# Column sums by products with ones, a longer run of idle-filling products, and four subtractions moved from VectorE to GpSimd

## The chip, the cores and the metric

The kernel runs on one core of one Trainium2 chip. The metric is the device time of one execution in microseconds; lower is better. The engines are named as in the profile: PE is TensorE (PEld its weight loads), DVE is VectorE, ACT is ScalarE, POOL is GpSimd, and SP is the queue that issues most DMAs.

## What is computed

One residual decoder layer on 1024 tokens of width 1024, all in float32. Only its front is touched by the change:

```python
mod = (c_act @ w_ada[l] + b_ada[l])[:, None, :]
sh1, sc1, g1, sh2, sc2, g2 = jnp.split(mod, N_MOD, axis=-1)
h = rms_norm(h_res, norm1_g[l]) * (1.0 + sc1) + sh1
proj = h @ w_in[l]          # columns: q 512 | k 128 | v 128 | u 512
...                         # q, k, v: windowed attention; u: pooling means
h_res = h_res + g1 * mixed
h2 = rms_norm(h_res, norm2_g[l]) * (1.0 + sc2) + sh2
ff = jnp.square(jax.nn.relu(h2 @ w_mlp_in[l])) @ w_mlp_out[l]
h_res = h_res + g2 * ff
```

## The kernel before

The order of every engine's work is written out by hand; semaphores join the engines. Nothing is reordered by a scheduler: an instruction that waits holds up all that stands behind it on its engine.

**The modulation.** The vector c is laid out as 128 partitions by 8. The loop over `n` on DVE adds 16 pieces of `w_ada` (128x1024 each, one `add_piece` per piece, L1164 and L1166): the first eight into `acc` (shift, sh1), the other eight into `squares` (scale, sc1, the last of them in two halves, L1206). Each piece arrives by a DMA from SP. What is then missing is the sum over the 128 partitions. `turn_sums` on PE transposes `acc` or `squares` in 128x128 blocks into PSUM (L1965), and DVE sums each block along its rows by TENSOR_REDUCE (L1219 for the shift, L1226 for each half of the scale, inside `scale_1`) and adds the bias columns `cols` (L1221, L1228). L1231 forms `a1 = (1 + scale) * norm_g`.

**The input.** ACT scales the first two 128-token tiles of x (`xh`, L709), PE transposes each (`turn_x`, 8 transposes), DVE and ACT apply `a1` and `b1` to one half each (`make_h` L1240, `make_h_half` L718), ACT rounds the result to `fp32r` (`hi_h` L728) and DVE subtracts to get the low part (`lo_h` L1246). The weights are split in the same way: ACT casts (`hi_wu` L733 for the four pieces of the u columns, 128x1024 each; `hi_wqkv` L737 for the eight pieces of the q, k, v columns, 128x768 each), and DVE subtracts (`lo_wu` L1253, `lo_wqkv` L1259). Every projection is three products, hi*hi, hi*lo and lo*hi (L1969 to L1971), per 128 rows of weights.

**The order on PE.** `turn_sums(acc)`, `keep_clock(8)`, `turn_x(0)`, `turn_x(1)`, `keep_clock(6)`, `turn_sums` for each half of `squares`, `keep_clock(14)`, then `project_u(0)` (24 products; its steps wait for `h_lo` and, two steps each, for one `wu_lo`), the q projection (24 products, step k waits for `wqkv_lo` k+1), the k and v projection, and `project_u(1)`. `keep_clock(n)` is n products of `ident` by `ident` into a PSUM bank that nobody reads; each is two records in the trace, while a transpose is one.

**The order on DVE behind the modulation.** `scale_1(0)`, `make_h(0,0)`, `scale_1(1)`, `lo_wu(0)`, `lo_h(0,0)`, `lo_wu(1)`, `lo_h(0,1)`, `lo_wu(2)`, `lo_wu(3)`, four `lo_wqkv`, `make_h(1,0)`, four `lo_wqkv`, two `lo_h` of the second tile. **On ACT:** `hi_wu(0)`, `hi_wu(1)`, `hi_h(0,0)`, `make_h_half(0)`, `hi_h(0,1)`, `hi_wu(2)`, `hi_wu(3)`, five `hi_wqkv`, `make_h_half(1)`, and so on. **On POOL:** masks and pooling bands, the root for the first two tiles (L1823, L1825), then nothing until the q and k norms of the first tile.

Of the kernel before, what the change touches and what calls it, by code (L numbers as in the profile page):

```python
# [16 lines left out]
P = 128  # L17
F32 = mybir.dt.float32
# [3 lines left out]
ALU = mybir.AluOpType  # L22
ACT = mybir.ActivationFunctionType
AX_X = mybir.AxisListType.X
# [11 lines left out]
SH1, SC1, G1, SH2, SC2, G2 = range(6)  # L36
# [17 lines left out]
def build(nc, x, c, positions, w_ada, b_ada, norm1_g, w_in, q_norm_g, k_norm_g, attn_sinks,  # L54
          pool_w, pool_scale, w_o, norm2_g, w_mlp_in, w_mlp_out, out):
    S, D = x.shape[1], x.shape[2]
    IN = w_in.shape[2]
# [9 lines left out]
    KD = D // P  # L67
# [5 lines left out]
    QKV = AW + 2 * KVW  # L73
# [11 lines left out]
    with ExitStack() as ctx:  # L85
# [3 lines left out]
        def sb(name, shape, dt=F32):  # L89
            return ctx.enter_context(nc.sbuf_tensor(name, shape, dt))  # L90
# [4 lines left out]
        def over(name, shape, at, dt=F32):  # L95

            with ExitStack() as hold:
                if at:
                    hold.enter_context(nc.sbuf_tensor(name + "_below", [P, at // 4], F32))
                return hold.enter_context(nc.sbuf_tensor(name, shape, dt))  # L100

        ident = sb("ident", [P, P])
        ones = sb("ones", [P, P])
        small = sb("small", [P, 256])
        cols = sb("cols", [P, 72])
        a1, b1, a2, b2 = (small[:, 8 * j:8 * j + 8] for j in range(4))
# [23 lines left out]
        acc = over("acc", [P, D], AT_ACC)  # L130


        with ExitStack() as mix_ctx:
# [4 lines left out]
            wih = mb("w_in_hi", [P, KD, IN], F32R)  # L138
            wil = mb("w_in_lo", [P, KD, IN], F32R)
# [66 lines left out]
        psum = ctx.enter_context(nc.psum_tensor("psum", [P, 8, 512], F32))  # L206
# [4 lines left out]
        def bank(j):  # L211
            return psum[:, j, :]

        def banks(j):
            return psum[:, j:j + 2, :].rearrange("p b n -> p (b n)")
# [52 lines left out]
        mod_turned = sem("mod_turned")  # L268
        sc1_turned = sem("sc1_turned")
        mod_taken = sem("mod_taken")  # L270

        a1_ready = sem("a1_ready")
        wu_hi, wu_lo = sem("wu_hi"), sem("wu_lo")
# [180 lines left out]
        def landed(eng, piece):  # L454

            n = place[piece]
            buf, use, _ = buffer_of(n)
            eng.wait_ge(raw_in[buf], 16 * use)
            return piece_at(n)
# [54 lines left out]
        acc_sc = squares[:, :]  # L514
# [634 lines left out]
        def _(dve):  # L1149
            own_d = Chain(dve, own["dve"])  # L1150
            v = nc.vector
# [43 lines left out]
            for n in range(2 * KD):  # L1195
                if n >= 1:
                    dve.wait_ge(mod_summed, n)
                if n < KD:
                    add_piece(acc[:, :], ("sh1", n), n, mod_summed)
                elif n < 2 * KD - 1:  # L1200
                    add_piece(acc_sc, ("sc1", n - KD), n - KD, mod_summed)
                else:
                    a = landed(dve, ("sc1", KD - 1))
                    for h in range(2):
                        cut = slice(512 * h, 512 * h + 512)
                        v.scalar_tensor_tensor(out=acc_sc[:, cut], in0=a[:, cut], scalar=silu[:, KD - 1:KD],  # L1206
                                               in1=acc_sc[:, cut], op0=ALU.mult, op1=ALU.add).then_inc(mod_summed, 1)
                if n == 4:
                    dve.wait_ge(rows_in, 16 * 4)
                    v.tensor_copy(rows[64:72, :], posi[64:72, :]).then_inc(posf_ready, 1)  # L1210
                if n == KD + 2:

                    dve.wait_ge(rows_turned, 1)
                    v.tensor_copy(cols[:, :], psum[:, 4, 0:72]).then_inc(cols_ready, 1)
                if n == 2 * KD - 4:

                    dve.wait_ge(cols_ready, 1)
                    dve.wait_ge(mod_turned, 1)
                    v.tensor_reduce(b1, banks(0).rearrange("p (k n) -> p k n", n=P), AX_X, ALU.add).then_inc(mod_taken, 1)  # L1219
                    dve.wait_ge(mod_taken, 1)  # L1220
                    own_d.step(v.tensor_tensor(b1, b1, cols[:, 8 * SH1:8 * SH1 + 8], ALU.add))  # L1221
            def scale_1(h):

                c4 = slice(4 * h, 4 * h + 4)
                dve.wait_ge(sc1_turned, h + 1)
                own_d.step(v.tensor_reduce(a1[:, c4], bank(2 + h).rearrange("p (k n) -> p k n", n=P), AX_X, ALU.add))  # L1226
                own_d.wait()
                own_d.step(v.tensor_tensor(a1[:, c4], a1[:, c4],  # L1228
                                           cols[:, 8 * SC1 + 4 * h:8 * SC1 + 4 * h + 4], ALU.add))
                own_d.wait()  # L1230
                v.scalar_tensor_tensor(out=a1[:, c4], in0=a1[:, c4], scalar=1.0, in1=cols[:, 48 + 4 * h:52 + 4 * h],  # L1231
                                       op0=ALU.add, op1=ALU.mult).then_inc(a1_ready, 1)
# [14 lines left out]
                                xh[:, t % 2, 512 * h:512 * h + 512].rearrange("p (k n) -> p k n", n=P),  # L1247
                                hT(t)[0][:, 4 * h:4 * h + 4, :].bitcast(F32), ALU.subtract).then_inc(h_lo, 1)

            def lo_wu(j):  # L1250
                a = landed(dve, ("wu", j))
                dve.wait_ge(wu_hi, j + 1)
                v.tensor_tensor(wil[:, 2 * j:2 * j + 2, QKV:IN], a.rearrange("p (k n) -> p k n", k=2),  # L1253
                                wih[:, 2 * j:2 * j + 2, QKV:IN].bitcast(F32), ALU.subtract).then_inc(wu_lo, 1)

            def lo_wqkv(k):
                a = landed(dve, ("wqkv", k))
                dve.wait_ge(wqkv_hi, k + 1)
# [2 lines left out]
            scale_1(0)  # L1261
            make_h(0, 0)
            scale_1(1)
            lo_wu(0)
            lo_h(0, 0)
            lo_wu(1)
            lo_h(0, 1)
            lo_wu(2)
            lo_wu(3)
            for k in range(4):  # L1270
                lo_wqkv(k)
            make_h(1, 0)
# [491 lines left out]
        def _(pool):  # L1764
            own_p = Chain(pool, own["pool"])
            g = nc.gpsimd
# [64 lines left out]
            pool.wait_ge(x_squared, 2)  # L1831
            root(rx[:, 0:2], ssx[:, 0:2], D, x_root)

            def lo_wo(k):
                pool.wait_ge(wo_hi, k + 1)
                g.tensor_tensor(wol[:, k, :], piece_at(place[("wo", k)]), woh[:, k, :].bitcast(F32),
                                ALU.subtract).then_inc(wo_lo_pool, 1)
# [123 lines left out]
        def _(pe):  # L1961
            mm = nc.tensor.matmul
# [16 lines left out]
            def keep_clock(n, at):  # L1979

                for _ in range(n):
                    mm(psum[:, at, 0:P], ident[:, :], ident[:, :], start=True, stop=True)

            def turn_sums(o, sums):

                for k in range(o.shape[1] // P):
                    ins = tr(o[:, k * P:(k + 1) * P], sums[:, k * P:(k + 1) * P])
                return ins
# [114 lines left out]
            tr(psum[:, 4, 0:72], rows[0:72, :], 72).then_inc(rows_turned, 1)  # L2103

            pe.wait_ge(mod_summed, KD)
            turn_sums(banks(0), acc).then_inc(mod_turned, 1)
            pe.wait_ge(mod_summed, 2 * KD - 5)
            keep_clock(8, 2)
            turn_x(0)
            pe.wait_ge(cols_ready, 1)  # L2110
            turn_x(1)
            keep_clock(6, 2)
            for h in range(2):
                pe.wait_ge(mod_summed, 2 * KD + h)
                turn_sums(bank(2 + h), acc_sc[:, 512 * h:512 * h + 512]).then_inc(sc1_turned, 1)
            pe.wait_ge(mod_taken, 1)
            keep_clock(14, 0)

# [216 lines left out]
            for h in range(2):  # L2335
                if h == 1:
                    pe.wait_ge(h2_lo_last, 2)
                for b in range(2):
                    for c_ in ("C12", "C22"):
                        ins = head_half(b, c_, "A" + c_[1] + str(h + 1), late, NK * h, h == 0, h == 1)  # L2340
# [5 lines left out]
            for b in range(HEAD, NBLK):  # L2346
                for name in UP_NEXT:
                    up_product(b, name)
                    n = b - HEAD - KD - 1
# [56 lines left out]
```

## Time and profile before

| | us |
|---|---|
| three runs | 964.04, 964.57, 966.05 |
| median | 964.57 |
| the profiled execution, own time | 966.11 |
| its span in the trace | 964.4 |
| PE busy | 925.0 (96%) |
| DVE busy | 657.4 (68%) |
| ACT busy | 492.3 (51%) |
| POOL busy | 352.6 (37%) |

The profiled execution's own time lies 1.7 above its span and 1.5 above the median. A matmul's end is modelled in the trace, so a busy PE may still wait; its starts are what to read. In a row, the time before the bracket is the group's start and how long it lasted from its first start to its last end; the bracket holds the engine's idle time just before it and who ended that.

### The profile page before, as it was taken

The numbers are of one execution on the slowest core, as the hardware profiler recorded it, in microseconds if no ns is written. First come the engines' busy times: TensorE is split into PE (matmuls) and PEld (weight loads), VectorE is DVE, ScalarE is ACT, GpSimd is POOL, SyncE is SP. The second block draws the span as 40 slices with busy tenths as digits, with TensorE's granted clock in tenths as the row PEclk, the third lists the DMA queues.
The fourth block names the chain that finished last, engine by engine and source line by source line (L and its number), as shares of the span: only waits on it lengthen the run. The fifth ranks groups of instructions, "written<-read, shape, count | busy, mean of one in ns | idle before, by whom it ended". The sixth has DMA issues, their size and how long they took to land.

```text
span 964.4 us, 12633 instructions
## 1 busy us (share of the span) xinstructions
PE 925.0 (96%) x4411; PEld 765.2 (79%) x4411; DVE 657.4 (68%) x1000; ACT 492.3 (51%) x874; POOL 352.6 (37%) x342
## 2 busy tenths in 40 slices
PE   1898999998999999999999999999999999999998
PEld 1787788886778888787888788888888888888887
DVE  6876887878644687665556544535786666779896
ACT  1656777778464564644554455454443444333331
POOL 8032222215232443988888877851000000000000
DMA  9852332214222240665456533538999637987673
GB/s 360 298 170 93 131 110 79 78 64 153 89 88 87 88 154 22 222 213 176 154 169 210 177 132 133 173 138 276 351 345 333 226 99 239 308 307 245 227 252 113
DMA packets 92271, 175.54 MB, mean 182 GB/s; under 512 B 9320, under 2 KB 26288, under 8 KB 92208
## 3 DMA queue, kind: packets, MB, share of 16 engines
q1 hardware_dynamic: 92096, 174.70, 53.1%
q8 instruction: 35, 0.57, 0.2%
q14 instruction: 28, 0.23, 0.1%
q10 hardware_dynamic: 112, 0.04, 0.0%
HBM read 136.95 MB, written 37.75 MB: 181 GB/s over the span
## 4 chain that ended last, share of the span: by engine, by line
PE 84%; DVE 6%; ACT 5%; POOL 3%; issue 2%; DVEq 0%; POOLq 0%; ACTq 0%
PE psum L1969 26%; PE psum L1971 25%; PE psum L1970 25%; PE psum L1965 3%; ACT probs L780 2%; PE psum L2045 1%; PE psum L2068 1%; ACT probs L788 1%; POOL band L1788 1%; PE psum L2095 1%; PE psum L2026 1%; PE psum L2023 1%; PE psum L2024 1%; ACT qT L799 1%; DVE probs L1297 1%
## 5 line engine op out<-in xcount | busy, mean ns | idle before, releaser
L1076 ACT CAST down_operands<-down_raw 128x1024 fp32r<-128x1024 f32 x96 | 100.9, 1054 | 153.4 <-PE psum L1971 58.1
L1969 PE MATMUL psum<-down_operands 128*128 128x512 f32 x448 | 174.3, 389 | 0.0
L1970 PE MATMUL psum<-down_operands 128*128 128x512 f32 x448 | 174.3, 389 | 0.0
L1971 PE MATMUL psum<-down_operands 128*128 128x512 f32 x448 | 174.3, 389 | 0.0
L1705 DVE TENSOR_TENSOR down_operands<-down_raw,down_operands 128x1024 fp32r<-128x1024 f32 x93 | 112.5, 1219 | 19.1 <-ACT down_operands L1076 18.5
L1969 PE MATMUL psum<-h2T,w_operands 128*128 128x512 f32 x272 | 107.5, 395 | 1.9 <-DVE act_quads_a L1649 1.3
L1971 PE MATMUL psum<-h2T,w_operands 128*128 128x512 f32 x272 | 105.9, 390 | 0.0
L1970 PE MATMUL psum<-h2T,w_operands 128*128 128x512 f32 x272 | 105.9, 389 | 0.0
L1921 POOL TENSOR_TENSOR w_operands<-raw,w_operands 128x512 fp32r<-128x512 f32 x56 | 83.2, 1487 | 42.1 <-ACT w_operands L1028 42.1
L1969 PEld LDWEIGHTS psum<-down_operands 128*128 128x128 f32 x448 | 84.1, 188 | 17.6
L1970 PEld LDWEIGHTS psum<-down_operands 128*128 128x128 f32 x448 | 84.1, 188 | 17.4
L1971 PEld LDWEIGHTS psum<-down_operands 128*128 128x128 f32 x448 | 84.1, 188 | 17.3
L1823 POOL TENSOR_SCALAR small<-small 128x1 f32<-128x1 f32 (+2 forms) x23 | 8.3, 359 | 169.1 <-DVE small L1366 131.7
L1971 PE MATMUL psum<-t_sums_hi,w_operands 128*128 128x512 f32 x168 | 65.4, 389 | 0.0
L1969 PE MATMUL psum<-t_sums_hi,w_operands 128*128 128x512 f32 x168 | 65.4, 389 | 0.0
L1970 PE MATMUL psum<-t_sums_lo,w_operands 128*128 128x512 f32 x168 | 65.4, 389 | 0.0
L1969 PE MATMUL psum<-w_in_hi,hT_hi 128*128 128x512 f32 (+1 forms) x168 | 61.7, 368 | 2.7 <-DVE hT_lo L1246 1.7
L1969 PEld LDWEIGHTS psum<-h2T,w_operands 128*128 128x128 f32 x272 | 51.1, 188 | 15.8 <-issue 3.8
L1921 POOL TENSOR_TENSOR w_operands<-w_sums,w_operands 128x512 fp32r<-128x512 f32 x42 | 55.9, 1343 | 11.8 <-ACT w_operands L1028 11.8
L1970 PEld LDWEIGHTS psum<-h2T,w_operands 128*128 128x128 f32 x272 | 51.1, 188 | 10.8 <-issue 0.5
L1971 PE MATMUL psum<-w_in_hi,hT_lo 128*128 128x512 f32 (+1 forms) x168 | 59.6, 355 | 0.0
L1971 PEld LDWEIGHTS psum<-h2T,w_operands 128*128 128x128 f32 x272 | 51.1, 188 | 10.7
(251 smaller groups left out, 1973.4 us busy)
## 6 DMA issues: line engine op xcount, KB each, us to landing
down_raw<-in_w_mlp_out SPq DMA_DIRECT2D x160, 256.0 KB, 4.3
down_raw<-act_scratch SPq DMA_DIRECT2D x112, 256.0 KB, 3.3
raw<-in_w_ada SPq DMA_DIRECT2D x32, 512.0 KB, 4.7
raw<-in_w_mlp_in SPq DMA_DIRECT2D x32, 512.0 KB, 4.9
act_scratch<-act_quads_a SPq DMA_DIRECT2D x64, 256.0 KB, 2.2
act_scratch<-act_quads_b SPq DMA_DIRECT2D x48, 256.0 KB, 3.6
slots<-in_w_ada SPq DMA_DIRECT2D x8, 512.0 KB, 10.5
xh<-in_x SPq DMA_DIRECT2D x8, 512.0 KB, 6.1
```

Source lines behind the costliest of these rows:

```text
L780: nc.scalar.activation(pr[:, kv, h, 0:w], pr[:, kv, h, 0:w], ACT.Exp, bias=negm[:, hh:hh + 1], scale=rq(i)[:, hh:hh + 1], accum_out=den[:, ...
L788: ins = nc.scalar.activation(pr[:, kv, h, 0:w], pr[:, kv, h, 0:w], ACT.Copy, scale=rden[:, kv * G + h:kv * G + h + 1])
L799: nc.scalar.copy(qT[r, :, :].rearrange("p (m e) q -> p m e q", e=2)[:, :, e, :], bank(1)[r, :].rearrange("p (m q) -> p m q", q=P))
L1076: nc.scalar.copy(o[:, 0, :, :], r[:, 0:2, :]).then_inc(op2_hi, 1)
L1297: ins = v.tensor_tensor_reduce(out=pr[:, kv, h, 0:w], in0=banks(4)[:, 256 * h:256 * h + w], in1=mask[:, m0:m0 + w], scale=1.0, scalar=-3e3 ...
L1705: v.tensor_tensor(o[:, 1, :, :], r[:, 0:2, :], f32(o[:, 0, :, :]), ALU.subtract).then_inc(op2_lo_dve, 1)
L1788: own_p.step(g.affine_select(out=cut, in_=cut, compare_op=ALU.is_ge, fill=0.0, base=base, pattern=[[1, n]], channel_multiplier=-1))
L1921: g.tensor_tensor(o[:, 1, :, :], quad, o[:, 0, :, :].bitcast(F32), ALU.subtract).then_inc(w1_lo, 1)
L1965: return nc.tensor.transpose(o, i, ident[0:rows_, 0:rows_])
L1969: mm(o, wh, ah, start=first, stop=False, skip_group_check=adds)
L1970: mm(o, wh, al, start=False, stop=False, skip_group_check=adds)
L1971: return mm(o, wl, ah, start=False, stop=last, skip_group_check=adds)
```

## The change

Four things are done.

- `column_sum` takes the place of `turn_sums` at the front: for each block of 128 columns one product with the block as the stationary operand and one column of `ones` as the moving one, which leaves the sums over the partitions in one PSUM column. DVE's three TENSOR_REDUCE go, and the bias is added straight from PSUM.
- DVE copies `cols` behind piece 7 instead of piece 10.
- On PE, `keep_clock(8)` ahead of `turn_x(0)` becomes `keep_clock(14)`, and `keep_clock(6)` behind `turn_x(1)` becomes `keep_clock(4)`.
- The four `lo_wu` go from DVE, where they stood between `scale_1(1)` and `lo_wqkv(0)`, to POOL, behind the root of the first two tiles.

```diff
-                if n == KD + 2:
+                if n == KD - 1:
                     dve.wait_ge(rows_turned, 1)
                     v.tensor_copy(cols[:, :], psum[:, 4, 0:72]).then_inc(cols_ready, 1)
...
-                    v.tensor_reduce(b1, banks(0).rearrange("p (k n) -> p k n", n=P), AX_X, ALU.add).then_inc(mod_taken, 1)
-                    dve.wait_ge(mod_taken, 1)
-                    own_d.step(v.tensor_tensor(b1, b1, cols[:, 8 * SH1:8 * SH1 + 8], ALU.add))
+                    v.tensor_tensor(b1.rearrange("p (h k) -> p h k", h=2), psum[:, 0:2, 0:4],
+                                    cols[:, 8 * SH1:8 * SH1 + 8].rearrange("p (h k) -> p h k", h=2),
+                                    ALU.add).then_inc(mod_taken, 1)
             def scale_1(h):
...
-                own_d.step(v.tensor_reduce(a1[:, c4], bank(2 + h).rearrange("p (k n) -> p k n", n=P), AX_X, ALU.add))
-                own_d.wait()
-                own_d.step(v.tensor_tensor(a1[:, c4], a1[:, c4],
+                if h == 0:
+                    dve.wait_ge(mod_taken, 1)
+                own_d.step(v.tensor_tensor(a1[:, c4], psum[:, 2 + h, 0:4],
                                            cols[:, 8 * SC1 + 4 * h:8 * SC1 + 4 * h + 4], ALU.add))
...
             scale_1(1)
-            lo_wu(0)
             lo_h(0, 0)
-            lo_wu(1)
             lo_h(0, 1)
-            lo_wu(2)
-            lo_wu(3)
...
             root(rx[:, 0:2], ssx[:, 0:2], D, x_root)
+            def lo_wu(j):
+                a = landed(pool, ("wu", j))
+                pool.wait_ge(wu_hi, j + 1)
+                g.tensor_tensor(wil[:, 2 * j:2 * j + 2, QKV:IN], a.rearrange("p (k n) -> p k n", k=2),
+                                wih[:, 2 * j:2 * j + 2, QKV:IN].bitcast(F32), ALU.subtract).then_inc(wu_lo, 1)
+            for j in range(KD // 2):
+                lo_wu(j)
...
+            def column_sum(o, sums, k):
+                return mm(o, sums[:, k * P:(k + 1) * P], ones[:, 0:1], start=True, stop=True)
...
-            turn_sums(banks(0), acc).then_inc(mod_turned, 1)
+            for k in range(KD):
+                ins = column_sum(psum[:, k // 4, k % 4:k % 4 + 1], acc, k)
+            ins.then_inc(mod_turned, 1)
             pe.wait_ge(mod_summed, 2 * KD - 5)
-            keep_clock(8, 2)
+            keep_clock(14, 2)
             turn_x(0)
             pe.wait_ge(cols_ready, 1)
             turn_x(1)
-            keep_clock(6, 2)
+            keep_clock(4, 2)
             for h in range(2):
                 pe.wait_ge(mod_summed, 2 * KD + h)
-                turn_sums(bank(2 + h), acc_sc[:, 512 * h:512 * h + 512]).then_inc(sc1_turned, 1)
+                for k in range(4):
+                    ins = column_sum(psum[:, 2 + h, k:k + 1], acc_sc, 4 * h + k)
+                ins.then_inc(sc1_turned, 1)
```

On PE, at the front of the program, before the change (xh is the scaled input, squares the scale sums, ident the identity):

```order
L1965 MATMUL psum<-ident,acc 128x128 x8
L1982 MATMUL psum<-ident 128x128 x8
L1965 MATMUL psum<-ident,xh 128x128 x16
L1982 MATMUL psum<-ident 128x128 x6
L1965 MATMUL psum<-ident,squares 128x128 x8
L1982 MATMUL psum<-ident 128x128 x14
```

and after it:

```order
L1984 MATMUL psum<-ones,acc 128x1 x8
L1981 MATMUL psum<-ident 128x128 x14
L1964 MATMUL psum<-ident,xh 128x128 x16
L1981 MATMUL psum<-ident 128x128 x4
L1984 MATMUL psum<-ones,squares 128x1 x8
L1981 MATMUL psum<-ident 128x128 x14
```

Six more products of `ident` stand ahead of the transposes of x, two fewer behind them, and the transposes of the sums are products of one column.

On DVE, from the bias of the shift to the first weights of q, k and v, the piece of the difference:

```order
-L1219 TENSOR_REDUCE small<-psum 128x8
-L1221 TENSOR_TENSOR small<-small,cols 128x8
+L1219 TENSOR_TENSOR small<-psum,cols 128x8
 L1166 SCALAR_TENSOR_TENSOR squares<-raw,small,squares 128x1024 x2
 L1206 SCALAR_TENSOR_TENSOR squares<-raw,small,squares 128x512 x2
-L1226 TENSOR_REDUCE small<-psum 128x4
-L1228 TENSOR_TENSOR small<-small,cols 128x4
+L1228 TENSOR_TENSOR small<-psum,cols 128x4
 L1231 SCALAR_TENSOR_TENSOR small<-small,cols 128x4
 L1240 TENSOR_SCALAR xh<-psum,small 128x128 x4
```

The reduces are gone. What follows `scale_1(1)` was, before:

```order
L1231 SCALAR_TENSOR_TENSOR small<-small,cols 128x4
L1253 TENSOR_TENSOR w_in_lo<-slots,w_in_hi 128x2x512
L1246 TENSOR_TENSOR hT_lo<-xh,hT_hi 128x512
L1253 TENSOR_TENSOR w_in_lo<-slots,w_in_hi 128x2x512
L1246 TENSOR_TENSOR hT_lo<-xh,hT_hi 128x512
L1253 TENSOR_TENSOR w_in_lo<-slots,w_in_hi 128x2x512 x2
L1259 TENSOR_TENSOR w_in_lo<-slots,w_in_hi 128x768 x4
```

and is now:

```order
L1231 SCALAR_TENSOR_TENSOR small<-small,cols 128x4
L1246 TENSOR_TENSOR hT_lo<-xh,hT_hi 128x512 x2
L1253 TENSOR_TENSOR w_in_lo<-slots,w_in_hi 128x768 x4
```

On POOL, the root of the first two tiles, and behind it the four moved subtractions ahead of the q and k roots:

```order
L1813 TENSOR_SCALAR small<-small 128x2
L1815 TENSOR_TENSOR small<-small 128x2
L1827 TENSOR_TENSOR w_in_lo<-slots,w_in_hi 128x2x512 x4
L1813 TENSOR_SCALAR small<-small 128x10
L1815 TENSOR_TENSOR small<-small 128x10
```

## Rows read from the trace of the kernel before

**Rows 1.** The page: busy time, share and instructions of the engines.
```profile
PE 925.0 (96%) x4411; PEld 765.2 (79%) x4411; DVE 657.4 (68%) x1000; ACT 492.3 (51%) x874; POOL 352.6 (37%) x342
```

**Rows 2.** Timeline of PE: start, us, operation, count, idle before and its releaser.
```profile
22.38 3.78 PE L1982 MATMUL psum<-ident 128*128 128x128 f32 x16 [4.08 <-DVE squares L1166]
26.80 3.68 PE L1965 MATMUL psum<-ident,xh 128*128 128x128 f32 x16 [0.64 <-ACT xh L709]
30.26 1.96 PE L1982 MATMUL psum<-ident 128*128 128x128 f32 x12
32.06 1.04 PE L1965 MATMUL psum<-ident,squares 128*128 128x128 f32 x8
32.94 3.29 PE L1982 MATMUL psum<-ident 128*128 128x128 f32 x28
37.97 0.50 PE L1969 MATMUL psum<-w_in_hi,hT_hi 128*128 128x512 f32 x1 [1.75 <-DVE hT_lo L1246]
...
47.60 0.50 PE L1969 MATMUL psum<-w_in_hi,hT_hi 128*128 128x512 f32 x1 [0.93 <-DVE w_in_lo L1259]
```

**Rows 3.** Windows: busy us (records) by engine, PE clock column, DMA share, GB/s.
```profile
30.00:31.00 1.00, 1.00 (x7) 1.00 (x6) 0.28 (x1) 0.90 (x1) 0.00 (x0) 1.00 1.06 389
31.00:32.00 1.00, 1.00 (x10) 1.00 (x10) 0.00 (x0) 0.14 (x1) 0.00 (x0) 1.00 1.06 395
```

**Rows 4.** Chain that ended last, 32 to 52 us: start, us, what.
```profile
32.70 0.70 DVE small L1226
...
33.62 0.17 DVE small L1231
...
33.82 1.36 DVE xh L1240 x4
...
38.37 1.90 ACT w_in_hi L733 x2
...
48.10 0.23 PE psum L1970
```

**Rows 5.** Timeline of DVE and ACT around the first tile.
```profile
24.89 1.22 DVE L1219 TENSOR_REDUCE small<-psum 128x8 f32<-128x1024 f32 x1
...
30.10 1.04 ACT L733 CAST w_in_hi<-slots 128x1024 fp32r<-128x1024 f32 x1 [0.31 <-DMA slots<-in_w_in]
...
36.21 1.51 ACT L718 ACTIVATE xh<-psum,small 128x128 f32<-128x128 f32 x4 [0.37 <-DVE small L1231]
37.75 0.62 ACT L728 CAST hT_hi<-xh 128x512 fp32r<-128x512 f32 x1
...
39.57 2.35 DVE L1253 TENSOR_TENSOR w_in_lo<-slots,w_in_hi 128x1024 fp32r<-128x1024 f32 x2
41.84 3.56 DVE L1259 TENSOR_TENSOR w_in_lo<-slots,w_in_hi 128x768 fp32r<-128x768 f32 x4
45.32 1.36 DVE L1240 TENSOR_SCALAR xh<-psum,small 128x128 f32<-128x128 f32 x4
46.60 3.55 DVE L1259 TENSOR_TENSOR w_in_lo<-raw,w_in_hi 128x768 fp32r<-128x768 f32 x4
```

**Rows 6.** Timeline, 222 to 242 us: POOL subtractions of 128x1024 beside DVE.
```profile
222.31 2.38 POOL L1836 TENSOR_TENSOR w_o_lo<-raw,w_o_hi 128x1024 fp32r<-128x1024 f32 x1 [0.44 <-ACT w_o_hi L810]
222.75 2.02 DVE L1348 TENSOR_TENSOR pooledT<-pooledT,carry 128x64 f32<-128x64 f32 x1 [1.79 <-ACT pooledT L850]
...
234.84 1.22 DVE L1332 TENSOR_TENSOR w_o_lo<-raw,w_o_hi 128x1024 fp32r<-128x1024 f32 x1
235.35 2.96 POOL L1836 TENSOR_TENSOR w_o_lo<-raw,w_o_hi 128x1024 fp32r<-128x1024 f32 x1 [1.44 <-ACT w_o_hi L810]
...
238.71 2.40 POOL L1836 TENSOR_TENSOR w_o_lo<-raw,w_o_hi 128x1024 fp32r<-128x1024 f32 x1 [0.41 <-ACT w_o_hi L810]
239.15 1.29 DVE L1282 TENSOR_TENSOR pT_lo<-psum,pT_hi 128x512 fp32r<-128x512 f32 x2 [0.61 <-ACT pT_hi L764]
240.58 1.60 DVE L1332 TENSOR_TENSOR w_o_lo<-raw,w_o_hi 128x1024 fp32r<-128x1024 f32 x1
```

More of the change, by code:

```diff
@@ L1248, in lo_h @@
                                 hT(t)[0][:, 4 * h:4 * h + 4, :].bitcast(F32), ALU.subtract).then_inc(h_lo, 1)
[L1250 to L1254, printed above, removed]
             def lo_wqkv(k):
```

## The prediction

> **What bounds the kernel now.** I read the busy times first: PE is busy 96% of the span and all others far less [rows 1], so time is won only where PE stands idle. The change touches the first 50 us alone, so I read PE's timeline there [rows 2]. Once the input projections begin at 37.97, PE has one gap left before 51: at 47.60, 0.93 us, ended by DVE's `lo_wqkv(4)`. From there the q projection follows DVE's last four subtractions, which end at 46.60 + 3.55 = 50.15 [rows 5]; behind them PE needs one more step, and then has its k, v and second u projections ready to run. So the end of `lo_wqkv(7)`, 50.15, is the point that matters: whatever moves it moves the rest. The chain of waits says the same: DVE's reduce and small operations, `make_h`, ACT's casts, then DVE's subtractions [rows 4, 5]. I call M the start of `make_h(0,0)`, 33.82 before [rows 4].
>
> **The column sums.** Each half of the scale now costs PE 4 products of two records, 8 in all, where 4 transposes stood. A transpose at the fast level takes (32.94 - 32.06)/8 = 0.11 [rows 2]. No row has a product with one moving column; its weight load is that of the neighbours, so 0.11 per record is my upper bound (0.9 per half, 0.45 more than before) and half of it the lower one, since less is streamed. I take 0.11. DVE loses the reduce of 0.70 ahead of M [rows 4] and one of 0.61 behind it; the 1.22 of the shift [rows 5] lies ahead of DVE's last pieces of the scale, which then end at 29.2 instead of 30.3. PE isn't there before 30, so that is worth nothing. The earlier copy of `cols` costs nothing either: it is the same 0.2 us on DVE, which waits for pieces there.
>
> **The clock.** The window table's clock column reads 1.00 all along and doesn't show it, the pace of the records does. Before: 16 transposes from 26.80 to 30.26, 0.216 each; 8 from 32.06, 0.11 each [rows 2]; the records per us go from 7 to 10 and 12 about 31.2 [rows 3]. 128 columns in 0.11 are the 2.4 GHz level, 0.216 for the same work 1.2 GHz. Before the rise PE had worked since 26.80 without a break (4.4 us), and since 22.38 with a break of 0.64. Now 28 records start at 22.38 and nothing breaks the run. I bound the rise by these two: 26.8, as long behind the start as it was behind the break, and 31.2, no earlier than before. I claim no fixed length; I take 26.8, as the break is what the change takes away. Then 20 records are slow (to 26.8) and 8 fast (27.6); 16 transposes at 0.11 end at 29.4, 8 records of `keep_clock(4)` at 30.2, 8 of the column sums at 31.1. Before, DVE began 0.3 behind the last transpose's start; the bias addition would start at 31.4 and L1231 0.2 later, at 31.6, against 33.62. For each us that the clock rises later, it comes about 0.5 later.
> The Trainium skill ("TensorE: Matmul & The Clock Gate", Part 4: PE-mode transpose) says that transposes don't count as activity for the clock. This trace speaks against it: of the 4.4 us before the rise, 3.5 were transposes. By the page the rise would hang on the `ident` products alone, of which there are more now; the sum above would stay.
>
> **The moved subtractions, and who they block.** POOL takes 2.38 and 2.40 for such a subtraction [rows 6]; DVE took 1.2. The point is what runs beside it. At 222.75 a DVE operation on 64 elements per partition, both inputs in SBUF, lasts 2.02: it ends when POOL's, begun at 222.31, ends (224.7). At 240.58 another lasts 1.60 instead of the 1.22 of its like at 234.84. The reverse too: POOL's operation at 235.35 lasts 2.96, as DVE's of 234.84 was running. DVE's operations at 239.15, with one input in PSUM, run at their usual 0.65 beside POOL [rows 6]. So DVE operations with two SBUF inputs and POOL's subtractions take turns. In `scale_1` that is L1231; and all of `lo_h` and `lo_wqkv`.
> First piece: ACT's cast ends at 29.8, POOL holds from 29.85 to 32.25. L1231 (asked for at 31.6) waits until 32.25, then POOL's second piece starts (its cast is done at 31.14 [rows 5]) and holds until 34.5. M becomes 32.3, 1.5 earlier than 33.82. `make_h(0,0)` 1.36 to 33.7; the second L1231, wanted at 33.9, waits until 34.5. ACT: `make_h_half` 1.5 to 36.05, cast 0.62 to 36.7, `hi_wu(2)` to 37.65, `hi_wu(3)` to 38.6 (1.90 for both [rows 4]), then the q, k, v casts at 0.75 to 0.8 (three quarters of 1.04 [rows 5]).
> From 37.7 on POOL and DVE share the lock: POOL's third piece to 40.1; `lo_wqkv(0)`, ready at 39.4, to 40.9; POOL's fourth, 2.25 of it held, to 43.15; `lo_wqkv(1)` to (3) at 0.8 to 0.9 each, 45.65; `make_h(1,0)` 1.36 to 47.0; the last four 3.55 [rows 5], to **50.5**. Against 50.15: 0.35 later. The 1.5 won at M, and the 4 x 1.2 taken off DVE, go to two POOL pieces held at 2.3 each and to ACT's casts, which are in no greater hurry than before (DVE now idles from 37.4 to 39.4, where it worked). `project_u(0)` waits for the fourth piece at 43.15 and ends at 43.15 + 6 x 0.23 (a product of 512 columns [rows 4]) = 44.6, 3 us before the q projection's fifth step needs its weights: covered. Past that nothing changes: behind the moved pieces POOL waits for the squares of q and k, which come after the q projection; and on SP's queue no load of x, parameters or modulation waits for `wu_lo`.
> The skill's page "SBUF — State Buffer" (Who interferes with whom) gives this as an exclusive lock of a whole instruction, for DVE operations with two SBUF inputs. It leaves the sum as it is.
>
> **Sum.** Span 964.4 + 0.35, own time 966.11 + 0.35; the profiled execution stands 1.54 above the median, so 964.57 + 0.35 = **964.9**. A measurement tells about 0.2%, 1.9 us, from no change.
>
> **Rival 1, slower: POOL's second piece gets ahead of L1231.** If DVE asks later than 32.25, POOL already holds for its second piece, and L1231 waits until 34.6. M is then 34.65, 2.35 later than in my forecast; the second L1231 no longer waits (0.6 saved at 34.5), which leaves `lo_wqkv(7)` at 50.5 + 1.85 = 52.35, 2.2 later than before: 966.8. It decides at a request of 32.25, that is a clock rise at 28.1 or later by the 0.5 per us. For it: the rise before came at 31.2, and my 26.8 rests on one instance. Against it: 1.3 us of margin, more if the column sums are cheaper. If the clock had not risen by 31.2 either, it would also be this case. Chance 0.26, of which about 0.17 come out over 1.9.
>
> **Rival 2, faster: no turns are taken.** If these POOL operations (rows of two strips of 512) don't block DVE, M is 31.8, `make_h_half` starts at M + 2.05, `hi_wu(2)` ends at M + 5.1 = 36.9, POOL's pieces at 36.9 + 2 x 2.4 = 41.7, and PE is bound by them: 6 products of `project_u(0)` (1.4) and 24 of q (5.5) end at 48.6, against 51.2: 2.6 earlier, 962.0. Against it stand the three pairs of [rows 6] with two SBUF inputs on DVE. Chance 0.08.
>
> **Rival 3: the turns cost less.** If POOL's hold is 1.9 instead of 2.3 (the 1.60 at 240.58 shows 0.15 released early) and casts keep pace, the result is 0.5 to 1.5 better than before: 963.1 to 964.1. Chance 0.16, in "same" nearly all.
>
> **Rival 4: the clock drops.** PE now idles 38.0 to 40.1 and 41.5 to 43.15, against 1.75 at most before, without a drop. If it fell, 18 products until 48 at 0.43 instead of 0.23 would cost 3.6, less the 0.7 of cover: 2.9, 967.8. Chance 0.04.
>
> **The numbers.** My forecast holds 0.46: 964.9, itself 964.2 to 965.6. Together: faster 0.10 (rival 2 and the edge of 3), slower 0.22 (rivals 1 and 4, and 0.01 of the rest), same 0.68. For 8 in 10 the range takes in rival 3 and most of rival 1 and leaves out rival 2 and the far end: 962.9 to 967.0.
>
> **What would show it.** In the changed trace: the pace of PE's records falls from 0.216 to 0.11 at about 26.8, within the first stretch of 28 or the transposes (else rival 1); the first L1231 lasts about 0.6 instead of 0.17 and ends with POOL's first piece, the second likewise with POOL's second; M at 32.3 or 34.6; `lo_wqkv(0)` lasts 1.5 or more; the last `lo_wqkv` ends at 50.5; PE's records from 51 on are shifted by the same amount as that end. I am wrong if DVE's operations beside POOL keep their lengths (rival 2), or if what follows 51 us takes up or returns a shift, for which I see no place.

## The result

Fourteen runs of each kernel: before 965.16 us median (964.04 to 966.52), changed 966.93 us median (966.63 to 969.21). The ratio is 1.0023 with a 95% interval of 1.0016 to 1.003: the change makes the kernel about 2.2 us slower (2.2 by the means of the fourteen, 1.8 by the medians). Eight of the changed kernel's runs lie between 966.63 and 966.97, the other six between 967.59 and 969.21. Forecast was 964.9 and no measurable difference, in a range of 962.9 to 967.0.

The profile of the changed kernel (own time 966.97, span 965.2). Page, part 1, which answers to [rows 1]:

```profile
PE 928.3 (96%) x4435; PEld 768.0 (80%) x4435; DVE 653.6 (68%) x993; ACT 492.1 (51%) x874; POOL 364.2 (38%) x346
```

PE's timeline at the front, which answers to [rows 2] (start, length of the group, count, idle before and its releaser):

```profile
22.45 5.80 PE L1981 MATMUL psum<-ident 128*128 128x128 f32 x28 [2.64 <-DVE squares L1166]
28.17 2.21 PE L1964 MATMUL psum<-ident,xh 128*128 128x128 f32 x16
30.21 1.06 PE L1981 MATMUL psum<-ident 128*128 128x128 f32 x8
31.11 1.84 PE L1984 MATMUL psum<-ones,squares 128*128 128x1 f32 x16
...
40.76 0.47 PE L1968 MATMUL psum<-w_in_hi,hT_hi 128*128 128x512 f32 x1 [1.83 <-POOL w_in_lo L1827]
...
43.72 0.80 PE L1968 MATMUL psum<-w_in_hi,hT_hi 128*128 128x512 f32 x1 [0.42 <-POOL w_in_lo L1827]
...
51.83 0.28 PE L1968 MATMUL psum<-w_in_hi,hT_hi 128*128 128x256 f32 x1
```

The 16 transposes of x take 2.21 instead of 3.68: the faster pace is there before they begin. PE now waits for POOL twice. The last row is the first product for k and v.

DVE and POOL, from the scale to the last weights of q, k and v, against [rows 4, 5]:

```profile
32.29 0.34 DVE L1231 SCALAR_TENSOR_TENSOR small<-small,cols 128x4 f32<-128x4 f32 x1
32.67 1.37 DVE L1240 TENSOR_SCALAR xh<-psum,small 128x128 f32<-128x128 f32 x4
...
34.14 0.81 DVE L1231 SCALAR_TENSOR_TENSOR small<-small,cols 128x4 f32<-128x4 f32 x1
...
39.88 6.34 DVE L1253 TENSOR_TENSOR w_in_lo<-slots,w_in_hi 128x768 fp32r<-128x768 f32 x4 [2.01 <-ACT w_in_hi L737]
46.14 1.36 DVE L1240 TENSOR_SCALAR xh<-psum,small 128x128 f32<-128x128 f32 x4
47.42 3.55 DVE L1253 TENSOR_TENSOR w_in_lo<-raw,w_in_hi 128x768 fp32r<-128x768 f32 x4
```

```profile
30.26 4.67 POOL L1827 TENSOR_TENSOR w_in_lo<-slots,w_in_hi 128x1024 fp32r<-128x1024 f32 x2 [3.32 <-ACT w_in_hi L733]
38.24 5.42 POOL L1827 TENSOR_TENSOR w_in_lo<-slots,w_in_hi 128x1024 fp32r<-128x1024 f32 x2 [3.32 <-ACT w_in_hi L733]
```

Four `lo_wqkv` (L1253 here) take 6.34 where they took 3.56 [rows 5], and POOL's two pieces beside them 5.42 instead of two times 2.4. The small L1231 takes 0.34 and 0.81 instead of 0.17: it ends when POOL's first and second piece end. The last `lo_wqkv` ends at 47.42 + 3.55 = 50.97, against 50.15.

So within this pair of traces the loss is 0.8, as the spans say (965.2 and 964.4). The means are 2.2 apart. The run of before that was traced (966.11) lies 0.85 above the mean of its fourteen, and that of the changed kernel (966.97) 0.47 below its own: 0.86 + 0.85 + 0.47 make the 2.2. The first of these two offsets is the main finding below; the second comes from the six longer runs.

### The profile page after: what moved, and what is told of

Same layout as the page of the kernel before. It is cut to its first block, busy times and chain, and to the rows that moved or that the text cites. A ratio compares the mean times of both kernels' runs of the same rounds, so it can differ in the third digit from the quotient of the medians.

```text
span 965.2 us, 12679 instructions
## 1 busy us (share of the span) xinstructions
PE 928.3 (96%) x4435; PEld 768.0 (80%) x4435; DVE 653.6 (68%) x993; ACT 492.1 (51%) x874; POOL 364.2 (38%) x346
## 4 chain that ended last, share of the span: by engine, by line
PE 84%; DVE 6%; ACT 5%; issue 2%; DMA 1%; POOL 1%; SPq 1%; DVEq 0%; ACTq 0%; POOLq 0%
PE psum L1968 26%; PE psum L1969 25%; PE psum L1970 25%; PE psum L1964 3%; ACT probs L780 2%; DMA slots<-in_w_ada 1%; PE psum L2047 1%; PE psum L2070 1%; ACT probs L788 1%; PE psum L1981 1%; PE psum L2097 1%; PE psum L2028 1%; PE psum L2026 1%; PE psum L2025 1%; ACT qT L799 1%
## 5 line engine op out<-in xcount | busy, mean ns | idle before, releaser
L1968 PEld LDWEIGHTS psum<-h2T,w_operands 128*128 128x128 f32 x272 | 51.1, 188 | 15.8 <-issue 3.9
L1969 PE MATMUL psum<-w_in_lo,hT_hi 128*128 128x512 f32 (+1 forms) x168 | 60.0, 357 | 0.0
L1969 PEld LDWEIGHTS psum<-h2T,w_operands 128*128 128x128 f32 x272 | 51.1, 188 | 10.8 <-issue 0.5
```

What stands on the lines that cost most here:

```text
L1968: mm(o, wh, ah, start=first, stop=False, skip_group_check=adds)
L1969: mm(o, wh, al, start=False, stop=False, skip_group_check=adds)
```

## The experiments

The measure in each trace is M, the start of `make_h(0,0)`, and E, the end of the last `lo_wqkv`. The k and v products start 0.85 to 0.88 behind E and the span ends 913.3 to 913.4 behind that (before: 51.00 and 964.4; changed: 51.83 and 965.2) in all traces but five, which are told where they come up; in those the clock falls on the way. The expectations argue with theories. A: DVE and POOL take turns, and the moved subtractions are the loss. B: the loss is in the rest of the change. C: the two engines don't block one another. D: without DVE's long reduce, POOL's root and so the scaling of x come late. E: the kernel before has two groups of times, since the pace of PE rises at two moments. F: a later fall of the clock makes the groups.

Each ratio is against runs of the kernel before on the same chip; M and E are of one trace each.

| kernel | median us (runs) | ratio to before, interval | M | E |
|---|---|---|---|---|
| before, first trace | 965.16 (14) | 1 | 33.82 | 50.15 |
| changed, first trace | 966.93 (14) | 1.0023 (1.0016, 1.003) | 32.67 | 50.97 |
| a_dve_lo | 964.20 (12) | 0.9995 (0.9985, 1.0005) | 35.11 | 50.83 |
| b_dummy | 968.38 (5) | 1.0036 (1.0023, 1.0048) | 32.63 | 52.37 |
| b_clock | 964.21 (11) | 0.9991 (0.9982, 0.9999) | 32.52 | 48.85 |
| a_clock_back | 968.64 (5) | 1.0036 (1.0024, 1.0048) | 34.76 | 52.64 |
| a_dve_root | 963.81 (10) | 0.9982 (0.9972, 0.9991) | 32.02 | 47.75 |
| a_root | 967.72 (10) | 1.0023 (1.0013, 1.0032) | 32.19 | 50.46 |
| b_sums | 966.19 (10) | 0.9999 (0.9983, 1.0015) | 33.96 | 49.69 |
| best | 961.86 (4) | 0.9959 (0.9944, 0.9974) | 29.69 | 45.41 |
| a_two_pool | 964.73 (10) | 0.9998 (0.9988, 1.0007) | 32.43 | 48.57 |
| b_pool_lo | 970.34 (4) | 1.0051 (1.0035, 1.0068) | 34.94 | 53.29 |

E less M separates the turns from what comes ahead of them. It is 16.3 in the traces of before and 15.7 with the column sums and all four `lo_wu` on DVE (a_dve_lo, a_dve_root, b_sums, best): a reduce less. With two pieces on POOL it is 16.1 (a_two_pool), with all four 18.3 (the changed kernel, a_root; 17.9 in a_clock_back, where the second L1231 isn't held). So behind M the move costs 2.6, of which the first two pieces are 0.4, and the column sums give back 0.6.

### The move alone, taken back and alone

**a_dve_lo:** the changed kernel with `lo_wu` on DVE again (the first two lines stand in POOL's program).

```diff
-            for j in range(KD // 2):
-                lo_wu(j)
...
             scale_1(1)
+            lo_wu(0)
             lo_h(0, 0)
+            lo_wu(1)
             lo_h(0, 1)
+            lo_wu(2)
+            lo_wu(3)
```

> The changed kernel with the four lo_wu back on VectorE, in their old places; column sums and the new clock-keeping counts stay. Theory A (VectorE and GpSimd take turns; the moved subtractions are the loss): L1231 of scale_1 lasts 0.17 again, make_h(0,0) starts at about 32.5, the last lo_wqkv ends at 48.6 instead of 50.97 in the changed kernel and 50.15 in the kernel before. So 1.5 us below the kernel before and 2.3 below the changed one: 963.6, ratio to before 0.9985. Theory B (the longer clock-keeping or the column sums are the loss, the move costs nothing): the time stays that of the changed kernel, 966.9, ratio 1.002.

Measured 964.20, eight of twelve runs between 963.56 and 964.27: 2.7 below the changed kernel. Theory B falls. The mean of its runs is only 0.5 below the kernel before, and the interval takes in 1. E of its trace, 50.83, is no proof of the forecast 48.6, since that trace is of the slowest run (968.02); its cause is told under the root.

**b_pool_lo:** the kernel before with the move alone (the same edit the other way).

> The kernel before with the move of the four lo_wu alone (transposes, reduces and clock-keeping of before). Theory A: where the clock rises late, L1231 comes behind GpSimd's first piece and waits for the whole second: make_h(0,0) at 35, last lo_wqkv at 53, 969.3; where it rises early, 967.2; so a median of 968 to 969 and a ratio of 1.003 to 1.0045, more than the full change loses. Rival: the move costs nothing by itself, 965.2, ratio 1.000.

Measured 970.34, 1.0051, the dearest of all, above the forecast 1.0045. In its timeline of DVE the two-input operation L1228 `small<-small,cols` is the one that is held:

```profile
32.44 0.69 DVE L1226 TENSOR_REDUCE small<-psum 128x4 f32<-128x512 f32 x1 [2.30 <-PE psum L1964]
33.16 1.54 DVE L1228 TENSOR_TENSOR small<-small,cols 128x4 f32<-128x4 f32 x1
34.74 0.17 DVE L1231 SCALAR_TENSOR_TENSOR small<-small,cols 128x4 f32<-128x4 f32 x1
```

The reduce, which reads PSUM, runs its usual 0.69; four elements per partition then take 1.54, to the end of POOL's second piece. This is rival 1. M and E are where theory A had them (35 and 53). What lies above the forecast is the clock: PE idles until 43.08 and 46.04 for POOL's third and fourth piece, the clock column falls, and the k and v products start 1.99 behind E instead of 0.86 (columns as in [rows 3]):

```profile
40.00:45.00 5.00, 2.89 (x11) 1.56 (x9) 2.99 (x3) 5.00 (x8) 4.42 (x2) 0.92 0.73 216
45.00:50.00 5.00, 3.99 (x10) 3.14 (x10) 5.00 (x8) 2.30 (x7) 0.99 (x1) 0.50 0.07 15
```

This is rival 4, with a price of 1.1. The change as a whole costs less than its move, because the other parts bring L1231 ahead of POOL's second piece, and because its clock is back in time.

**b_dummy:** the kernel before with two POOL subtractions that nobody needs and nobody waits for (`w_in_hi` minus itself into `acc`).

```diff
+            pool.wait_ge(mod_turned, 1)
+            for j in (2, 3):
+                pool.wait_ge(wu_hi, j + 1)
+                q = wih[:, 2 * j:2 * j + 2, QKV:IN].bitcast(F32)
+                own_p.step(g.tensor_tensor(acc[:, :].rearrange("p (k n) -> p k n", k=2), q, q, ALU.subtract))
+                own_p.wait()
```

> The kernel before, with two extra GpSimd subtractions of 128x1024 (w_in_hi minus itself, into acc, which nobody reads then), each after the cast of its u piece (3rd and 4th). They do no work for the result and nobody waits for them. Theory A: from 39.3 us on they take turns with VectorE's lo_wu and lo_wqkv, each holding VectorE for some 2.3 us: the last lo_wqkv ends 3.5 to 4.6 later than 50.15, and the time is 969 (ratio 1.004 to 1.0045). Theory C (the engines don't block one another there): 965.2, ratio 1.000, and each VectorE subtraction keeps its length of 0.95.

968.38, and the timeline has the blocking with nothing else changed:

```profile
38.28 4.78 POOL L1838 TENSOR_TENSOR acc<-w_in_hi 128x1024 f32<-128x1024 f32 x2 [12.02 <-ACT w_in_hi L733]
38.39 5.75 DVE L1253 TENSOR_TENSOR w_in_lo<-slots,w_in_hi 128x1024 fp32r<-128x1024 f32 x2
```

Two `lo_wu` take 5.75 instead of 2.35 [rows 5], 1.7 more for each of POOL's. Theory C falls. E, 52.37, is earlier than forecast (53.6 or later), since the forecast counted from the E of the first trace of before; with M at 32.63 a trace of before has its E at 49.0, and 3.4 are added, the 5.75 less 2.35.

**a_two_pool:** the changed kernel with pieces 0 and 1 on POOL, 2 and 3 on DVE.

```diff
             lo_h(0, 1)
+            dve.wait_ge(wu_lo, 2)
+            lo_wu(2)
+            lo_wu(3)
...
-            for j in range(KD // 2):
+            for j in range(2):
                 lo_wu(j)
```

> The changed kernel with only the first two lo_wu on GpSimd, the third and fourth back on VectorE behind lo_h(0,1). Theory A places the loss in the third and fourth piece, which fall among lo_wqkv, and only some 0.5 us in the first two (they hold back L1231 twice): the last lo_wqkv ends at 48.7 to 49.0 instead of 50.97, 964.8, ratio to before 1.000 or just under, 2.1 below the changed kernel. Rival: every piece on GpSimd costs alike: halfway between the changed kernel and that with all four on VectorE, 965.6.

964.73 and E 48.57: as theory A had it. By the medians pieces 2 and 3 cost 2.2. The 0.5 between 964.73 and 964.20 is not clear of noise (0.9998 and 0.9995, with intervals that overlap); for the first two pieces E less M says 0.4.

### The clock

**b_clock**, from the kernel before, has the edit below; **a_clock_back**, from the changed one, its reverse:

```diff
-            keep_clock(8, 2)
+            keep_clock(14, 2)
...
-            keep_clock(6, 2)
+            keep_clock(4, 2)
```

> The kernel before with keep_clock 14 and 4 in place of 8 and 6, nothing else. Theory A: TensorE's records reach the faster pace at about 27.5 in place of 31.2, VectorE's first L1226 starts at 31.8 instead of 32.7, and everything behind is 0.9 earlier: ratio 0.999, and the runs lie closer together than those of the kernel before (964.0 to 966.5), since there the pace rises behind a break. Theory B (the longer stretch is itself the loss): 0.5 to 2 us slower, ratio 1.001 to 1.002.

> The changed kernel with keep_clock 8 and 6 back. Theory A: the column sums end later, so that L1231 is asked for behind GpSimd's first piece and waits for the whole of its second: make_h(0,0) starts at 34.9 to 35.1 instead of 32.67, the last lo_wqkv ends at about 53: 2 us above the changed kernel, 969, ratio to before 1.004. Theory B (the longer stretch is the loss): faster than the changed kernel, back to the time of the kernel before, ratio 1.000.

The longer stretch alone gains some 0.9 us (0.9991, the interval below 1), and without it the changed kernel loses 1.3 more by the ratios (1.7 by the medians), in two intervals that overlap. In the trace of a_clock_back PE, with six products less to fill its time, idles 1.95 us for x. The pace falls in the middle of the transposes, at about 29.5, and is back at 32.9 (clock column 0.87 from 28 to 30 and 0.52 from 30 to 33):

```profile
27.97 2.74 PE L1964 MATMUL psum<-ident,xh 128*128 128x128 f32 x16 [1.95 <-ACT xh L709]
30.50 2.64 PE L1981 MATMUL psum<-ident 128*128 128x128 f32 x12
```

So L1231 comes late and is held until POOL's second piece ends:

```profile
34.17 0.55 DVE L1231 SCALAR_TENSOR_TENSOR small<-small,cols 128x4 f32<-128x4 f32 x1
34.76 1.36 DVE L1240 TENSOR_SCALAR xh<-psum,small 128x128 f32<-128x128 f32 x4
```

**b_look1 to b_look4, a_look1 and a_look2:** the two kernels unchanged, for more traces.

> The kernel before, unchanged, for a second trace. Its times fall into two groups, 964.0 to 964.8 and 965.7 to 967.0. Theory E: the groups are two moments at which TensorE's pace rises; a run of the lower group shows the faster pace at 27 to 28 us and make_h(0,0) at 32.6, one of the upper group 31 to 32 us and 33.8, as the first trace did. Rival: the front is alike in both and the difference lies later in the span.

> The same once more: theory E as for the first of the two; across all traces of the kernel before, the time goes with the start of make_h(0,0), 964.4 with 32.6 and 966.1 with 33.8.

> The kernel before, unchanged. If this run lies at 965.6 or above: theory E says make_h(0,0) at 33.8 or later and the clock column 1.00 between 150 and 230; theory F (a later fall of the clock) says make_h(0,0) at 32.2 to 32.4 and the column at 0.98 there. If it lies below 964.8, both say 32.2 to 32.4 and 1.00.

> The same once more: above 965.6, E says make_h(0,0) at 33.8 or later, F a column of 0.98 between 150 and 230 us; below 964.8 neither.

> The changed kernel, unchanged. In a run of 966.6 to 967.0 the last lo_wqkv ends at 50.5 to 51.0 and the k and v products start 0.9 behind it, with the column at 1.00 from 150 to 230. In one of 967.6 or above either GpSimd's second piece stood ahead of L1231 (make_h(0,0) at 34.6), or the clock was low beyond 45 us (k and v products 1.7 behind the last lo_wqkv), or the column is 0.98 between 150 and 230.

> The same once more, with the same three causes for a time of 967.6 or above.

| trace | us | faster pace from | M | E | k, v products | clock column, 150 to 230 |
|---|---|---|---|---|---|---|
| before, first | 966.11 | 31.3 | 33.82 | 50.15 | 51.00 | 1.00 |
| b_look1 | 964.60 | 27.4 | 32.38 | 48.71 | 49.56 | 1.00 |
| b_look2 | 964.54 | 25.8 | 32.22 | 48.55 | 49.41 | 1.00 |
| b_look3 | 964.60 | 27.3 | 32.30 | 48.63 | 49.48 | 1.00 |
| b_look4 | 966.46 | 31.5 | 34.17 | 50.50 | 51.36 | 1.00 |
| changed, first | 966.97 | 27.5 | 32.67 | 50.97 | 51.83 | 1.00 |
| a_look1 | 966.65 | 25.3 | 32.48 | 50.74 | 51.60 | 1.00 |
| a_look2 | 966.87 | 27.0 | 32.60 | 50.88 | 51.74 | 1.00 |

Theory E holds in all five traces of before. The kernel before has two fronts. PE's timeline of b_look2 and of b_look4:

```profile
22.66 3.48 PE L1982 MATMUL psum<-ident 128*128 128x128 f32 x16 [4.55 <-DVE squares L1166]
27.08 2.20 PE L1965 MATMUL psum<-ident,xh 128*128 128x128 f32 x16 [0.93 <-ACT xh L709]
```

```profile
22.80 3.78 PE L1982 MATMUL psum<-ident 128*128 128x128 f32 x16 [4.59 <-DVE squares L1166]
27.22 3.68 PE L1965 MATMUL psum<-ident,xh 128*128 128x128 f32 x16 [0.64 <-ACT xh L709]
```

With nearly the same starts, the 16 transposes take 2.20 in one and 3.68 in the other. The first trace of before [rows 2] is of the second sort. The changed kernel is of the first sort in all its three traces. So the 14 products do what they should, but what they give is already there in about half the runs of before (in the rounds of the runs above, 35 of 75 lie below 965).

### The root of the first two tiles

In the trace of a_dve_lo the two x tiles are scaled late. ACT, then PE:

```profile
28.17 2.19 ACT L709 ACTIVATE xh<-xh,small 128x1024 f32<-128x1024 f32 x2 [9.99 <-POOL small L1825]
```

```profile
22.33 5.13 PE L1982 MATMUL psum<-ident 128*128 128x128 f32 x28 [2.44 <-DVE squares L1166]
29.37 3.63 PE L1965 MATMUL psum<-ident,xh 128*128 128x128 f32 x16 [1.91 <-ACT xh L709]
```

The scaling started at 25.59 in the first trace of before and at 25.9 to 26.0 in the four others; in the three traces of the changed kernel it started at 26.8 to 27.0. POOL's root ahead of it reads SBUF, and without the reduce of 1.22 (PSUM only) DVE's two-input additions follow one another, so each of POOL's small operations waits for one. The last of them in b_look1, beside the reduce, and in the changed kernel, beside an addition:

```profile
25.27 0.72 POOL L1825 TENSOR_TENSOR small<-small 128x2 f32<-128x2 f32 x1
25.17 1.77 POOL L1815 TENSOR_TENSOR small<-small 128x2 f32<-128x2 f32 x1
```

The reduce is not all: in the trace of b_sums, which has none, POOL is one turn earlier and the scaling starts at 25.91. In a_dve_lo PE ran dry for 1.9 us. The pace had been fast since 26.0, fell again and was slow for the transposes; the clock column is 1.00 from 25 to 29 and 0.57 from 29 to 33.

**a_dve_root** and **a_root** make that root earlier, by the edit below (a_dve_lo and the changed kernel as their base). **b_sums** has no part of it: it is the kernel before with the column sums and the earlier copy of `cols` alone.

```diff
             for i, w in enumerate(POOL_WINDOWS):
+                if i == NP - 1:
+                    pool.wait_ge(x_squared, 2)
+                    root(rx[:, 0:2], ssx[:, 0:2], D, x_root)
...
-            pool.wait_ge(x_squared, 2)
-            root(rx[:, 0:2], ssx[:, 0:2], D, x_root)
```

> The changed kernel with lo_wu on VectorE and GpSimd's root of the first two tiles ahead of its last pooling band; nothing else. Theory D: x is scaled by 22 instead of 28 to 30, the transposes start behind the 14 clock-keeping products at 28.2 without a gap, make_h(0,0) at 32.3, the last lo_wqkv at 48.2: 963.3, and no runs above 965 as the kernel without the root's move had (966.5 and 968.0). Without D: the same as that kernel, 964.2 median with a tail to 968.

> The changed kernel (lo_wu on GpSimd) with the root of the first two tiles ahead of GpSimd's last pooling band; nothing else. Theory D: the casts start at 28.7 instead of 29.07 and GpSimd's first piece at 29.9 instead of 30.26; make_h(0,0) 0.3 earlier at 32.3, the last lo_wqkv 50.6 instead of 50.97: 966.5, and the tail of the changed kernel (967.6 to 969.2) goes. Theory A alone: 966.9 with its tail.

> The kernel before with the column sums and the earlier copy of cols alone; lo_wu stays on VectorE, clock-keeping 8 and 6. Theory D: the two reduces behind the scale save 1.3 us, but the scaling of x starts at 26.8 to 28 instead of 25.6 to 26.3, so the transposes and the scale sums come 1 to 2 later: no gain, 965 to 966.5, ratio 1.000 to 1.001. Rival: the reduces' saving stays: 964.0, ratio 0.9985.

a_dve_root: 963.81, all ten runs from 963.21 to 964.19, so the tail to 968 goes, as theory D had it. b_sums: 966.19, widely spread (962.49 to 968.81), ratio 0.9999: the column sums alone bring nothing that can be measured. That its trace has the early scaling (25.91) leaves open whether theory D is the reason.

a_root was a miss. M and E come 0.5 earlier, as expected or more, and two of its ten runs are at the forecast (966.52, 966.60), but the median is 967.72 and the ratio that of the changed kernel. The trace is of the slowest run (968.65). In its window table (columns as in [rows 3]):

```profile
40.00:45.00 5.00, 4.20 (x10) 2.93 (x11) 5.00 (x4) 4.34 (x9) 3.16 (x2) 0.58 0.58 187
45.00:50.00 5.00, 5.00 (x18) 3.92 (x17) 5.00 (x9) 2.98 (x5) 0.00 (x0) 0.74 0.20 45
```

and that of the changed kernel:

```profile
40.00:45.00 5.00, 3.82 (x10) 2.62 (x11) 5.00 (x3) 4.83 (x9) 3.66 (x2) 0.66 0.61 191
45.00:50.00 5.00, 5.00 (x22) 3.51 (x20) 5.00 (x9) 2.47 (x4) 0.00 (x0) 1.00 0.13 17
```

The clock column is the mean granted clock as a share of full speed; here it shows the fall to the lower level (1.2 of 2.4 GHz). PE had idled before, 1.83 us until 40.76 in the changed kernel, for POOL's third piece. There the clock is back before the k and v products, so it costs nothing (0.86 behind E). In a_root it is low to 47.6, and they start at 52.20, 1.74 behind its E: 0.9 us lost. This is rival 4. Another 1.3 are lost behind the k and v products, where the clock column differs in one stretch, first of a_root, then of the changed kernel:

```profile
225.00:233.00 8.00, 6.18 (x25) 5.07 (x26) 7.52 (x20) 6.58 (x15) 2.87 (x5) 0.79 0.44 146
225.00:233.00 8.00, 6.60 (x37) 5.64 (x38) 7.48 (x22) 6.59 (x15) 2.56 (x6) 1.00 0.54 166
```

Less the 0.5 won, the two make the 1.7 between 968.65 and 966.97. Which of them the seven runs from 967.63 to 967.99 have isn't shown.

### The version that beats both

**best:** column sums, `lo_wu` on DVE, the early root, and x transposed ahead of the 14 products.

```diff
-            pe.wait_ge(mod_summed, 2 * KD - 5)
-            keep_clock(14, 2)
             turn_x(0)
             pe.wait_ge(cols_ready, 1)
             turn_x(1)
-            keep_clock(4, 2)
+            keep_clock(14, 2)
```

> Built from the column sums with the four lo_wu on VectorE. Two further edits: GpSimd makes the root of the first two tiles ahead of its last pooling band instead of behind it, and TensorE transposes x before the 14 clock-keeping products, which now lie between x and the scale sums (the 4 are gone). Theory A with D (D: without the long reduce VectorE leaves GpSimd no room, so the root and with it the scaling of x come late, and x bounds TensorE's order): x is scaled by 22, the column sums of the scale start as soon as VectorE has them, 28.5, make_h(0,0) at 30.2, the last lo_wqkv ends at 45.8 to 46.5: 961.2 to 962, ratio to before 0.996. Rival: the weights of q, k and v are late or ScalarE's casts bind: last lo_wqkv at 48, 963.5.

961.86, 0.9959 (0.9944 to 0.9974). PE:

```profile
20.62 3.44 PE L1966 MATMUL psum<-ident,xh 128*128 128x128 f32 x16 [0.96 <-ACT xh L709]
23.90 3.29 PE L1983 MATMUL psum<-ident 128*128 128x128 f32 x28
28.21 1.95 PE L1986 MATMUL psum<-ones,squares 128*128 128x1 f32 x16 [1.01 <-DVE squares L1206]
```

The column sums now wait for DVE's last piece of the scale, not for PE's own order, and E is 45.41. Against a_dve_root, which differs by this edit alone, M and E are 2.3 earlier. The clock falls here too (the 28 records from 30.01 take 5.00, column 0.66 from 30 to 35), but DVE works without a break from 29.30 to E, so this costs E nothing.

## Why the prediction was wrong

- **What bounds the front: right.** In the thirteen traces without a fall of the clock that reaches the k and v products or comes later, the rest of the span follows E by the same amount (0.86 + 913.4).
- **The turns of DVE and POOL: right, a little small.** Forecast: L1231 held, M 32.3, `lo_wqkv(0)` 1.5 or longer, E 50.5. Measured: M 32.67, 1.55 for `lo_wqkv(0)`, E 50.97. Of the 0.47 missing, 0.4 are the later start of POOL's first piece (30.26 instead of 29.85): ACT's casts start behind the late scaling. I had priced the reduce of the shift at nothing; it was the gap in which POOL's root got on. b_dummy and b_pool_lo show the turns by themselves.
- **The clock: right for the changed kernel, wrong for before.** The pace rose at 27.5, 25.3 and 27.0 (forecast 26.8). But I took it that the break of 0.64 us keeps the clock of before low until 31. It does so in two traces of five; in three the fast pace is there at 25.8 to 27.4, in spite of a break of 0.9.
- **The sum: this is the step that failed.** "Span 964.4 + 0.35 ..., the profiled execution stands 1.54 above the median, so 964.57 + 0.35 = 964.9." It is 2.0 below the 966.93 measured: 0.5 are the later E, 1.54 this term. The 1.54 was not an offset of profiling: the trace was of a run with the late front (M 33.82, 966.11), and the median of three, 964.57, is by its time a run with the early one (the three traces of the early front are of 964.54 to 964.60). The 1.5 us won at M were set against the late front and then taken off the median of early ones, which had them already. Against b_look2 (M 32.22, E 48.55) the changed kernel's M is 0.45 later and its E 2.4 later: 964.54 and 966.97. By the same turns, the sum on that base would have been 964.57 + (50.5 - 48.55) = 966.5. The three times before the prediction, 964.04, 964.57 and 966.05, already lay 1.5 apart, and I didn't ask which group the trace was from.
- **Rival 1** (L1231 behind POOL's second piece) didn't happen in the changed kernel's three traces; it did in b_pool_lo (there L1228 was held) and a_clock_back. **Rivals 2 and 3** fell: POOL's hold was 2.3, not less. **Rival 4** happened, without a price in the first trace of the changed kernel, and cost 0.9 in a_root and 1.1 in b_pool_lo. Whether it makes that kernel's own tail (967.6 to 969.2) isn't shown; I have no trace of such a run.
- **Open:** four traces (a_dve_lo, b_clock, a_root, b_sums) end 1.2 to 1.3 us later behind the k and v products than the others do. All four have a clock column of 0.79 from 225 to 233 us, where the other fourteen have 1.00. What sets it off wasn't tried.

## What to carry to other kernels

Ask of a trace which group of the measured times it belongs to before adding a difference read from it to a median: a gain against a late instance is no gain over the usual run. When work goes from DVE to POOL, look at which DVE operations beside it read two inputs from SBUF: a small one on the critical path waits for the whole POOL operation, and a DVE operation that reads only PSUM may be the gap in which POOL's chain gets on. Fill the time ahead of a late input with work that is already ready (x's transposes), and put the clock-keeping products behind it, not ahead: here this was worth 2.3 us of E (best against a_dve_root).

## What the runs showed of the hardware

A product with one moving column is no cheaper than a full one of 128 here: 16 records of `ones` take 1.84 us at the faster pace, 0.11 each, as the `ident` products do (28 records in 3.37).

A POOL operation that reads SBUF and a DVE operation with two SBUF inputs exclude one another here, down to 4 elements per partition on DVE's side (0.81 and 1.54 instead of 0.17) and 2 on POOL's (1.77 instead of 0.72), and they alternate when both queue (5.75 for two of 1.2). The Trainium skill, "SBUF — State Buffer", Who interferes with whom, names this pair as one that contends for a shared port that is locked exclusively; these rows agree.

The clock's rise is not fixed to the work ahead of it: with the same 16 records from 22.7 or 22.8 on and a break before 27.1 or 27.2, it came at 25.8 in one run (b_look2) and at 31.5 in another (b_look4). In b_pool_lo it came at 30.5, behind 16 transposes in a row (26.93 to 30.39).

Nor is its fall: behind an idle stretch of 1.83 us it fell in one trace of the changed kernel (column 0.66), and behind 1.78 and 1.79 it stayed up in the two others (1.00). In best it fell at 30.5, with only 1.01 us of idle time just ahead of the column sums at 28.21.
